# The second block's layer loop written out on three engines of a one-core Trainium2 kernel

## The reference

```
def second_block(x, ...):
    for layer in range(DEPTH_2):                      # DEPTH_2 = 2
        h = rms_norm(x, norm_mix_pre[layer])
        m = mixer_block(h, ...[layer])                # convolution, retention, gated linear attention, gates
        x = x + rms_norm(m, norm_mix_post[layer])
        h = rms_norm(x, norm_ffn_pre[layer])
        f = swiglu(h, w_ffn_gate[layer], w_ffn_up[layer], w_ffn_down[layer])
        x = x + rms_norm(f, norm_ffn_post[layer])
```

## Time and profile before

| | us |
|---|---|
| median of 3 runs | 2556.1 (2552.29 to 2562.09) |
| the profiled execution | 2548.08 |
| its span, first to last instruction | 2546.3 |
| PE busy | 2305.4 |
| DVE busy | 761.9 |
| ACT busy | 633.3 |

### The profile page before, as it was taken

The page is one execution under the profiler, slowest core; times in us unless marked ns, Lnnn a source line. Parts: engine busy times, 40 slices in busy tenths (PEclk is TensorE's granted clock), DMA queues, the critical chain, the costliest instruction groups (busy, mean ns, idle before and its releaser), DMA issues.

```text
span 2546.3 us, 31390 instructions
## 1 busy us (share of the span) xinstructions
PE 2305.4 (91%) x13190; PEld 1587.2 (62%) x13190; DVE 761.9 (30%) x1245; ACT 633.3 (25%) x884; POOL 44.7 (2%) x35
## 2 busy tenths in 40 slices
PE   4999997869988988898899889999899899998998
PEld 2468666643333333333333359998799799987997
DVE  1001224251111111111111155444354455442453
ACT  2101342031111111111111134441343435412432
POOL 2100000010000000000000000000000000000000
PEclk8997999869999999999999989999899899998999
DMA  9433353329999999999999967672254444541442
GB/s 279 71 132 132 132 200 119 100 103 429 428 428 427 428 428 428 427 428 427 427 428 427 428 193 173 154 225 107 100 177 161 145 156 150 192 166 67 170 170 92
DMA packets 133834, 626.99 MB, mean 246 GB/s; under 512 B 9344, under 2 KB 17040, under 8 KB 108864
## 3 DMA queue, kind: packets, MB, share of 16 engines
q1 hardware_dynamic: 128672, 622.51, 64.6%
q0 software_dynamic: 2912, 1.44, 1.2%
q10 hardware_dynamic: 2112, 0.99, 0.2%
HBM read 623.69 MB, written 1.05 MB: 245 GB/s over the span
## 4 chain that ended last, share of the span: by engine, by line
PE 71%; DMA 20%; DVE 3%; issue 3%; ACT 2%; ACTq 0%; SPq 0%; DVEq 0%
DMA ring<-in_w_lin 18%; PE bank L1322 14%; PE bank L1057 13%; PE bank L1420 11%; PE bank L1620 10%; PE bank L1635 4%; PE bank L1072 2%; DMA ring<-in_w_ada 1%; PE bank L1444 1%; PE bank L1123 1%; PE bank L1429 1%; DMA ring<-in_w_in 1%; PE bank L1310 1%; PE bank L1335 1%; PE bank L1144 1%
## 5 line engine op out<-in xcount | busy, mean ns | idle before, releaser
L1322 PE MATMUL bank<-ring,arenaA 128*64 128x512 f32 x3072 | 693.1, 601 | 38.7 <-DMA ring<-in_w_lin 27.7
L1322 PEld LDWEIGHTS bank<-ring,arenaA 128*64 128x64 f32 x3072 | 211.0, 138 | 461.9 <-issue 390.4
L1057 PE MATMUL bank<-arenaA,ring 128*128 128x256 f32 (+1 forms) x1408 | 341.6, 402 | 14.5 <-ACT arenaA L669 9.2
L2038 DVE TENSOR_TENSOR ring_rounded<-ring,ring_rounded 128x2048 fp32r<-128x2048 f32 (+1 forms) x140 | 293.3, 2132 | 118.1 <-ACT ring_rounded L837 118.1
L1057 PEld LDWEIGHTS bank<-arenaA,ring 128*128 128x128 f32 x1408 | 269.9, 194 | 88.4 <-issue 38.1
L837 ACT ACTIVATE ring_rounded<-ring 128x2048 fp32r<-128x2048 f32 (+1 forms) x140 | 243.1, 1783 | 300.4 <-DMA ring<-in_w_in 80.3
L1420 PE MATMUL bank<-arena_rounded,ring_rounded 128*128 128x256 f32 x2496 | 308.9, 283 | 0.7 <-DVE ring_rounded L2038 0.7
L1420 PEld LDWEIGHTS bank<-arena_rounded,ring_rounded 128*128 128x128 f32 x2496 | 300.9, 190 | 5.0 <-issue 2.8
L1620 PE MATMUL bank<-arena_rounded,ring_rounded 128*128 128x256 f32 x2112 | 259.3, 286 | 2.2 <-ACT arena_rounded L962 2.2
L1620 PEld LDWEIGHTS bank<-arena_rounded,ring_rounded 128*128 128x128 f32 x2112 | 257.4, 193 | 4.2 <-ACT arena_rounded L962 2.7
L1984 DVE TENSOR_SCALAR arenaA<-bank 128x512 f32<-128x512 f32 x32 | 22.1, 691 | 506.7 <-PE bank L1322 506.7
(11 more groups left out here) (350 smaller groups left out, 1734.1 us busy)
## 6 DMA issues: line engine op xcount, KB each, us to landing
ring<-in_w_gate SPq DMA_DIRECT2D x64, 2048.0 KB, 23.2
ring<-in_w_lin SPq DMA_DIRECT2D x64, 2048.0 KB, 25.6
ring<-in_w_down SPq DMA_DIRECT2D x64, 2048.0 KB, 21.5
ring<-in_w_in SPq DMA_DIRECT2D x41, 2048.0 KB, 10.7
ring<-in_w_ada SPq DMA_DIRECT2D x12, 2048.0 KB, 15.4
ring<-in_w_ffn_gate SPq DMA_DIRECT2D x10, 2048.0 KB, 7.8
ring<-in_w_ffn_up SPq DMA_DIRECT2D x10, 2048.0 KB, 7.7
ring<-in_w_ffn_down SPq DMA_DIRECT2D x12, 1536.0 KB, 6.5
```

The lines of the kernel that those rows point to most:

```text
L1057: last = pe.matmul(dst, w[:, c, base + m * P:base + (m + 1) * P], rhs(c), start=(c == 0), stop=(c == kc - 1))
L1322: last = pe.matmul(bank[b][k * SLOTS:(k + 1) * SLOTS, :], lhsT(c), slot(j)[:, c % 4, k * 512:(k + 1) * 512], start=False, stop=(c == DC - ...
L2038: dve.tensor_tensor(place2(name, ringR)[:, a:b, :], w[:, a:b, :], hi[:, a:b, :], ALU.subtract).then_inc(w_lo, 1)
```

## The change

The hardware loop over the second block's two layers becomes a Python loop on PE, ACT and DVE. Each of the three programs then holds the body twice, one after the other, with no register for the layer and no branch between; every wait of the body compares with a constant, and three slices that were picked by the register become fixed slices. The order of the instructions on each engine, the work of each, the semaphores and SP's program stay as they were.

```
@@ scalar
-            with act.Fori(0, 2) as L:
+            for L in range(2):
...
-                act.activation(gaH, gaRaw[:, bass.DynSlice(L, 1), :].rearrange("p l (c n) -> p (l c) n", c=DC), ACT.Copy).then_inc(m_hi, 1)
+                act.activation(gaH, gaRaw[:, L:L + 1, :].rearrange("p l (c n) -> p (l c) n", c=DC), ACT.Copy).then_inc(m_hi, 1)
@@ tensor
-            with pe.Fori(0, 2) as L:
+            for L in range(2):
@@ vector
-            with dve.Fori(0, 2) as L:
+            for L in range(2):
...
-                link(dve.tensor_copy(v2c[:, :], v2T[:, :].rearrange("p (l n) -> p l n", l=2)[:, bass.DynSlice(L, 1), :]
+                link(dve.tensor_copy(v2c[:, :], v2T[:, :].rearrange("p (l n) -> p l n", l=2)[:, L:L + 1, :]
...
-                dve.tensor_tensor(gaL, gaRaw[:, bass.DynSlice(L, 1), :].rearrange("p l (c n) -> p (l c) n", c=DC),
+                dve.tensor_tensor(gaL, gaRaw[:, L:L + 1, :].rearrange("p l (c n) -> p (l c) n", c=DC),
```

## The result

The changed kernel takes 2561.25 us (median of 22 runs, 2555.46 to 2569.11), the kernel before 2556.13 us (22 runs, 2551.13 to 2563.79). The ratio is 1.0020, with a 95% interval of 1.0012 to 1.0029: 5 us slower, where 3.5 us faster had been forecast. It is within 0.5%, where the prediction had most of its chance, but the sign is clear, and the time lies 1.25 us above the range.

What follows compares the result with a forecast made beforehand. PE's own work was taken to bound the kernel (busy 91% of the span), with stalls between the layers as the removable excess. Only the border's 3.5 us counted: 2556.1 - 3.5 = 2552.6 us, range 2543 to 2560 us.

Steps and rivals of the forecast that it cites:

- ACT's branch, gain 3.5 us: Border between the second block's layers: removing ACT's 5.92 us stall shortens the 14.72 us chain by 3.5 us, up to 4.7.
- 11.20 us be the model and not 10.04: Border's expected length: as in mid layer two, with PE at its low clock (gain 3.52 us), not mid layer one (4.68).
- All three branches must go: Border: ACT's stall covers those of PE (until 2016.96) and DVE (until 2021.5); the gain needs all three removed.
- Is what ACT needs there? ... I count nothing.: Border: slab `rq` lands some 2.5 us before ACT needs it, 10.7 us being the usual load time; counted as nothing.
- rival 2: Border: no gain, the 6 us return as another wait, such as a late `rq` load; 2556 us, chance 0.10.
- The register instructions: Inside layers: 192 additions ahead of PE's waits become constants; off the path, counted as nothing, bounds 6.1 and 17 us.
- The page against the row: Branch back: a fetch stall of about 6 us, against a documented compare-and-branch of about 108 ns making the change worth 0.1 us.
- The longer program: Second layer written out: fetching straight code, 29 packets a layer, costs nothing, as layer one takes 497.3 us against 497.6.
- Rival 3: Inside layers: slower, straight code fetched late, each PE stall up to 6.66 us; 2559.3 us with one, chance 0.05.
- The range: Whole kernel: 2543 to 2560 us, from a gain of 0 to 6 us and median noise of 4 or 5 us.

Runs made afterwards that it cites:

- the two kernels with the other source: Kernel before and changed kernel, each layer's 16 mixer slabs read from `w_ffn_gate_2` instead of `w_in_2`: 2543.96 us with the loop, 2540.62 us written out.
- Written out with 576 KB: Changed kernel plus an input of 589824 bytes, ahead of all others, that no instruction reads: 2549.56 us (0.9977), repeated 2550.03 us (0.9978).
- the two controls: Kernel before and changed kernel, each run again unchanged: 2553.14 us (ratio 1.0001) and 2559.22 us (ratio 1.0016).
- the kernel with the long tail: Kernel before, loops kept, with 3600 one-column matmuls added behind PE's last work: 4089.52 us, read only for its loads.

## Why the prediction was wrong

The steps, in their order.

*ACT's branch, gain 3.5 us.* Right. 3.45 us in the profile, 3.0 us between the two kernels with the other source, where the medians differ by 3.3 us. That the low clock would hold through the border, and thus 11.20 us be the model and not 10.04, was right too: the granted clock was 0.57 there.

*All three branches must go.* Right in kind: with ACT's alone gone, the border lost only 0.5 us of its 14.7.

*"Is what ACT needs there? ... I count nothing."* Wrong in its number, with no effect on the sum. The slab `rq` landed 15.2 us after its issue, not 10.7, and ACT waited 1.85 us for it, as rival 2 described. But rival 2 had every microsecond of such a wait take one from the gain, and none was taken. The first square started 2.67 us behind DVE's first residual, where ahead of layer one it was 1.98 us; the last square started 4.32 us behind it in both places, since it has to wait for the residual. Written out with 576 KB, where ACT has no such wait, the border takes 11.26 us, as much as with it.

*The register instructions.* Right: groups of 48 matmuls take 5.70 us, and with the other source a layer up to its feed-forward part is only 1 to 1.5 us shorter.

*The page against the row.* Right: the stalls of about 6 us went with the branches. By the Trainium skill (Runtime: NRT & Kernel Launch, Instruction fetch mechanics) a taken branch to code that the engine doesn't hold waits for a fetch; the trace agrees, with 6.66 us on PE before and no such stall after. The compare-and-branch of about 108 ns (the Trainium skill, Advanced Engine Details and Errata, Control Flow Timing) is not what a branch back over a layer cost here.

*"The longer program ... costs nothing that I can see, and I take nothing."* This is the step that failed. I priced a longer program by fetching it, and fetching did cost nothing. I did not ask what else its length does. The sum carried every load time of before over to the changed kernel as if it were a property of the load; it is a property of the load in this program. The term left out measured +9.5 us in layer one and +3.6 us in layer two of the profiled execution: 13.1 us, against 3.45 us won. The size varies with the execution: in the profiles of the two controls the layers lost 5.9 and 4.6 us and the border won 3.3, and the medians of 22 runs, 5.1 us apart, leave about 8.6 us for the loss. Rival 3 named the right sign for another reason: no idle time without a releaser appeared on PE, and its waits lead back to loads.

*The range.* Noise is not what missed it: the median of the kernel before moved by 0.03 us from 3 to 22 runs. By the prediction's own terms, a gain of 0 to 6 us and 5 us of noise, the range would have been 2545 to 2561 us, and the 2561.25 us lie above that too.

Shown are: the loads repeat for a program, but for single slabs; they change when PE's program is made longer, with the loop kept too, and even for code that runs last; they change with an input that nobody reads; alone they depend on the first column; and with other loads the change gains 3.3 us. That the common cause is the place of `w_in_2` in device memory is the reading that fits these, but the traces show no addresses: it is argued and not shown, and something else that moves with the program and the inputs is not ruled out. The place within 4096 bytes can't be all of it: written out with 576 KB, the odd slabs are the slow ones in layer one and the fast ones in layer two, a whole multiple of 4096 bytes further. Open is whether PE's program or all programs together count, by what rule the place is chosen (64 KB, tried in the written-out kernel, and 448 KB, tried in the one with the loop, changed nothing; 576 KB did, in both directions), and why rows 32832 bytes apart are so sensitive and the rows of `w_ffn_gate_2`, 11264 bytes apart, were not.

## What to carry to other kernels

When a change alters the length of a program, look in the profile after at the loads first, also at those issued before the changed code: a load whose time differs there tells that it isn't what the code does when it runs. A difference of a few tenths of a per cent says little of an edit until its loads are the same in both kernels; take them from a source that is not sensitive, or move the data, and compare again. And of several stalls at one place, ask for each what stands behind it: removing one of three here was worth a sixth of removing all.

## What the runs showed of the hardware

A load of 1024 rows of 2048 bytes, 32832 bytes apart, took 9.7 to 15.3 us by its first column and layer, with nothing beside it, while loads of the same size from rows 11264 bytes apart, in the kernels with the other source, took 7.6 us in the median. A longer program on PE, or an unread input of 576 KB, moved the odd slabs of layer one between 10 and 15 us, and the time of the whole from 0.2% less to 0.5% more. A branch back over a layer held each of PE, ACT and DVE for about 6 us (6.66 us on PE, 8.1 us in the kernel with the long tail). Where PE had waited for a late slab, its granted clock stood at 0.50 for the next matmuls, and a group of 48 took 7.5 us in place of 5.7.
